# The weighted sum of expert value rows: from half VectorE, half TensorE to TensorE alone

## Chip, core and metric

The kernel runs on one core of a Trainium2 chip. The metric is the device time of one execution in microseconds (us), the median of three runs. All data is fp32.

## What is computed

A two-layer decoder trunk over 256 tokens of width 1024, batch 1. Layer 0 mixes tokens with sparse attention and retention, layer 1 with a convolution module; behind each stands a PEER layer, and at the end a norm. The change touches PEER, in which every token picks 16 experts in each of 8 heads out of 16384, and every expert is one row of `u` and one of `v`:

```python
def block(args):
    xb, ib, gb = args                       # 128 tokens, their 128 picks, their gates
    hb = jnp.einsum('td,tkd->tk', xb, u[ib])
    act = jax.nn.gelu(hb, approximate=False) * gb
    return jnp.einsum('tk,tkd->td', act, v[ib])
```

The picks come from a routing step: queries (`h @ w_q`), scores against 2 x 128 keys, top 16 of each half, top 16 of the sums, softmax.

## The kernel before

**Phases and rounds.** Tokens lie on the 128 partitions, in two tiles. There are four PEER phases p: layer 0 tile 0, layer 0 tile 1, layer 1 tile 0, layer 1 tile 1. A phase has 128 picks, in 8 rounds of RING = 16, a round in 4 batches of BATCH = 4. Every engine has its own program, and semaphores order them.

**One pick.** GpSimd (POOL) issues an indirect DMA that gathers for each token its expert's row, `u` and `v` side by side (2048 fp32, 1 MB for 128 tokens), into slot r of `ring` (L414); at most AHEAD = 5 are under way, and a slot must be free. VectorE makes the dot product with `h_tok` (L892). After four dots ScalarE makes gelu, multiplies by the gate (L566) and writes four diagonal matrices `diag` (L573), eight of which exist. The weighted row is added to the token's sum in two halves: VectorE adds columns 0 to 511 to `x_tok` (`add_v`, L900), four picks behind its dots; TensorE multiplies the diagonal with columns 512 to 1023 and accumulates in PSUM in `acc` (L1284), opened by `open_sum` (L1277) with the identity times `x_tok`, and copied back by `close_sum` (L915). A slot is free when `v_added` and `v_multiplied` have both counted it.

**What runs beside the rounds.** In phase 0 (from round 0), and in the rounds 4 to 7 of phases 1 and 2, the routing of the next picks is made two heads at a time. In TensorE's program a piece stands behind each batch: query 0 behind batch 0, query 1 behind batch 1, scores 0 behind batch 2, scores 1 behind batch 3 (`heads_in_steps`, L1266; products L1042, scores L1263). VectorE's `heads` (L811) stands behind the round's dots and additions and begins with the maxima over both heads' scores (L822); the next round's dots stand behind it. In rounds 0 and 1 of phase 0 TensorE also makes two of the four products of the attention's output projection for tile 1, behind batches 2 and 3, and VectorE adds them (`add_projected`) ahead of round 2. Rounds 0 to 3 of phases 1 and 2 hold the convolution of a tile: TensorE's `conv_in` makes 8 channel tiles behind batches given by CONV_INS, ScalarE their gates by CONV_GATES (L584), VectorE a `conv_pair` of 31 taps for two channel tiles (L931, L943) between rounds or, for pairs 1 and 3, ahead of pick 8 of round 1 and pick 12 of round 2; then mean, variance, norm, and four products `conv_out` with the second weight in round 3. Phase 3 has only picks. Weights (1 MB chunks of 256 columns) come on SyncE's queue into two buffers `wbuf` (L328), each load waiting for the product of the chunk two before it.

Of the kernel before, what the change touches and what calls it, by code (L numbers as in the profile page):

```python
# [6 lines left out]
P = 128  # L7
D = 1024
KD = D // P
# [29 lines left out]
HALF = D // 2  # L39
# [29 lines left out]
def hybrid_decoder_trunk_kernel(nc, x, gains, w_in, kv_norm, uk_t, uv_w, w_o, rot, decay,  # L69
# [13 lines left out]
    with ctx:  # L83
# [125 lines left out]
        acc = side[:, 2, :]  # L209
        cand = side[:, 3, :].rearrange("p (h a b) -> p h a b", h=2, a=P_TOP)  # L210
        pm = ctx.enter_context(nc.psum_tensor("pm", [P, 4 * 512], f32))
# [23 lines left out]
        wo_ps = sem("wo_ps")  # L235
# [5 lines left out]
        dots_ready, act_ready, diag_ready, v_added, v_multiplied = (sem(n) for n in ("dots_ready", "act_ready", "diag_ready", "v_added", "v_multiplied"))  # L241
# [17 lines left out]
        wo_at = [[side_flat[:, c * 512:c * 512 + WCOLS] for c in range(4)], [pm[:, c * 512:c * 512 + WCOLS] for c in range(4)]]  # L259
# [104 lines left out]
        def _(pool):  # L364
# [22 lines left out]
            def gathers(p):  # L387
# [3 lines left out]
                with pool.Fori(0, rounds // 2) as i:  # L391
                    for half in range(2):
                        r0 = p * rounds + half
                        pool.wait_ge(picks_ready, i * 2 + (r0 + 1))
                        pool.wait_ge(v_added, i * (2 * RING) + (r0 * RING + 1))
# [4 lines left out]
                        for r in range(RING):  # L400
                            freed = r0 * RING + r + 1
                            pool.wait_ge(v_added, i * (2 * RING) + freed)
# [20 lines left out]
        def _(act):  # L423
# [155 lines left out]
            def gate_of_glu(t, n):  # L579

                c = n % 4
                act.wait_ge(pw_ps, t * KD + n + 1)
                act.wait_ge(glu_ready, t * KD + n + 1)
                act.activation(gate_sig[:, c, :], pm[:, c * 512 + P:c * 512 + 2 * P], ACT.Sigmoid,  # L584
                               bias=chan_sb[:, CP_BG + n:CP_BG + n + 1]).then_inc(sig_ready, 1)
# [69 lines left out]
        def _(dve):  # L655
# [12 lines left out]
            dve.sem_inc(glu_ready, 4)  # L668
            dve.sem_inc(v_added, RING)
# [114 lines left out]
            def add_projected(t, c):  # L784
# [3 lines left out]
                dve.tensor_tensor(xs, xs, wo_at[t][c], ALU.add)  # L788
# [94 lines left out]
            def expert_round(p, i, between=None):  # L883
# [4 lines left out]
                xs = x_tok[:, t, 0:HALF]  # L888

                def dot(r):  # L890
# [4 lines left out]
                def add_v(r):  # L895
                    n = p * PICKS + r
                    if r % BATCH == 0:
                        dve.wait_ge(act_ready, i * RING + (n + BATCH))
                    dve.wait_ge(v_added, i * RING + (n + RING))
                    dve.scalar_tensor_tensor(out=xs, in0=ring[:, r, D:D + HALF], scalar=act_v[:, r:r + 1], in1=xs,  # L900
                                             op0=ALU.mult, op1=ALU.add).then_inc(v_added, 1)

                for r in range(RING + BATCH):
                    if between:
                        between(r)
                    if r < RING:
                        dot(r)
                    if r >= BATCH:
                        add_v(r - BATCH)  # L910

            def close_sum(p):

                dve.wait_ge(v_multiplied, RING + (p + 1) * PICKS)
                dve.tensor_copy(x_tok[:, p % 2, HALF:D], acc).then_inc(x_ready, 1)  # L915

# [9 lines left out]
            def conv_pair(t, q):  # L926

                tiles = range(2 * q, 2 * q + 2)
                for c in tiles:
                    dve.wait_ge(sig_ready, t * KD + c + 1)  # L930
                    dve.scalar_tensor_tensor(out=glu[:, c, HIST:HIST + P], in0=pm[:, (c % 4) * 512:(c % 4) * 512 + P],  # L931
                                             scalar=chan_sb[:, CP_BA + c:CP_BA + c + 1], in1=gate_sig[:, c % 4, :],
                                             op0=ALU.add, op1=ALU.mult).then_inc(glu_ready, 1)
                for w in range(TAPS):
                    for c in tiles:
                        src, dst = glu[:, c, w:w + P], y_t[:, c, :]
                        tap = chan_sb[:, CP_DW + c * TAPS + w:CP_DW + c * TAPS + w + 1]
                        if w == 0:
                            dve.wait_ge(glu_ready, 4 + t * KD + c + 1)
# [26 lines left out]
            def conv_out(t):  # L966
# [5 lines left out]
                for c in range(4):  # L972
                    n = 4 * t + c
                    dve.wait_ge(w2_ps, n + 1)
                    xs = x_tok[:, t, c * WCOLS:(c + 1) * WCOLS]
                    dve.tensor_tensor(xs, xs, pm[:, c * 512:c * 512 + WCOLS], ALU.add)
# [14 lines left out]
            heads(0, 1)  # L991
            expert_round(0, 1)
            heads(0, 2)
            for c in range(4):
# [35 lines left out]
        def _(pe):  # L1030
# [171 lines left out]
            def output_product(t, c):  # L1202
                pe.wait_ge(a_ready, t + 1)
                pe.wait_ge(b_t_ready, t + 1)
                w = chunk(W_O[t] + c + (t and c // 2 * 2))
# [67 lines left out]
            def open_sum(p):  # L1273
# [3 lines left out]
                pe.matmul(acc, ident[:, :], x_tok[:, p % 2, HALF:D], start=True, stop=False)  # L1277

            def expert_round(p, i, between=None, last=False):

                for r in range(RING):
                    n = p * PICKS + r
                    pe.wait_ge(diag_ready, i * RING + (n + 1))
                    pe.matmul(acc, diag[:, r % (2 * BATCH), :], ring[:, r, D + HALF:2 * D],  # L1284
# [147 lines left out]
```

## Time and profile before

| | us |
|---|---|
| median of 3 runs | 1746.88 |
| lowest, highest | 1746.08, 1751.19 |
| span of the profiled execution | 1750.9 |
| VectorE busy | 1428.1 (82%) |
| TensorE busy (matmul) | 1002.7 (57%) |
| GpSimd, ScalarE busy | 775.9 (44%), 498.4 (28%) |
| DMA | 625.78 MB, 357 GB/s over the span |

DVE is VectorE, PE TensorE (PEld its weight loads), ACT ScalarE, POOL GpSimd, SPq SyncE's DMA queue. A square bracket at the end of a timeline row gives the idle time of the engine just before it and what ended it.
### The profile page before, as it was taken

The numbers are of one execution on the slowest core, as the hardware profiler recorded it, in microseconds if no ns is written. First come the engines' busy times: TensorE is split into PE (matmuls) and PEld (weight loads), VectorE is DVE, ScalarE is ACT, GpSimd is POOL, SyncE is SP. The second block draws the span as 40 slices with busy tenths as digits, with TensorE's granted clock in tenths as the row PEclk, the third lists the DMA queues.
The fourth block names the chain that finished last, engine by engine and source line by source line (L and its number), as shares of the span: only waits on it lengthen the run. The fifth ranks groups of instructions, "written<-read, shape, count | busy, mean of one in ns | idle before, by whom it ended". The sixth has DMA issues, their size and how long they took to land.

```text
span 1750.9 us, 17116 instructions
## 1 busy us (share of the span) xinstructions
PE 1002.7 (57%) x3934; PEld 610.9 (35%) x3934; DVE 1428.1 (82%) x3330; ACT 498.4 (28%) x1442; POOL 775.9 (44%) x565
## 2 busy tenths in 40 slices
PE   7998663555443653465455555355644456555655
PEld 7785442333331331333333333133422332222222
DVE  2755594999999889894999999988599999877776
ACT  2222220333222522232223242223222233222222
POOL 0003431434434578852344448874333345544551
PEclk9999777787777886676777777678777777776777
DMA  9147989799999999898999998899899998999996
GB/s 356 55 133 301 410 303 366 290 379 385 385 384 402 420 364 368 315 393 318 408 389 378 402 371 338 323 341 418 310 382 395 406 394 335 422 422 422 422 422 266
DMA packets 149994, 625.78 MB, mean 357 GB/s; under 512 B 9648, under 2 KB 76976, under 8 KB 84400
## 3 DMA queue, kind: packets, MB, share of 16 engines
q0 software_dynamic: 73728, 536.90, 75.7%
q1 hardware_dynamic: 76208, 88.20, 14.8%
q8 instruction: 24, 0.39, 0.1%
q14 instruction: 34, 0.28, 0.0%
HBM read 624.02 MB, written 1.05 MB: 357 GB/s over the span
## 4 chain that ended last, share of the span: by engine, by line
DVE 43%; PE 20%; DMA 17%; issue 11%; ACT 4%; DVEq 3%; ACTq 1%; POOL 0%; POOLq 0%
DVE ring L892 15%; DMA ring<-experts_dram,idx_now 11%; DVE x_tok L900 9%; PE pm L1042 9%; PE side L1284 7%; DVE conv_buf L943 7%; DMA wbuf<-w_o_dram 3%; DMA wbuf<-w_dram 3%; ACT act_v L566 1%; PE side L1042 1%; DVE top_i L825 1%; DVE rest L826 1%; DVE top_i L838 1%; ACTq L569 1%; DVE best_i L844 1%
## 5 line engine op out<-in xcount | busy, mean ns | idle before, releaser
L414 POOL DMA_INDIRECT ring<-experts_dram,idx_now x512 | 745.4, 1456 | 633.5 <-DMA ring<-experts_dram,idx_now 247.1
L1284 PE MATMUL side<-ring,diag 128*128 128x512 f32 x1024 | 597.0, 737 | 555.7 <-ACT diag L573 555.6
L892 DVE SCALAR_TENSOR_TENSOR ring<-ring,h_tok 128x1024 f32<-128x1024 f32 x512 | 615.7, 1220 | 55.8 <-DMA ring<-experts_dram,idx_now 50.7
L1284 PEld LDWEIGHTS side<-ring,diag 128*128 128x128 f32 x1024 | 232.6, 239 | 863.9 <-ACT diag L573 625.4
L900 DVE SCALAR_TENSOR_TENSOR x_tok<-ring,act_v,x_tok 128x512 f32<-128x512 f32 x512 | 383.8, 750 | 26.1 <-ACT act_v L566 20.3
L562 ACT ACTIVATE ge<-hb 128x4 f32<-128x4 f32 x128 | 26.3, 205 | 701.3 <-DVE ring L892 701.3
L573 ACT ACTIVATE diag<-ident,act_v 128x128 f32<-128x128 f32 x512 | 163.8, 390 | 15.9 <-issue 2.2
L397 POOL COPY idx_now<-eidx 128x16 uint32 x32 | 24.3, 760 | 258.1 <-DVE x_tok L900 184.3
L943 DVE SCALAR_TENSOR_TENSOR conv_buf<-conv_buf,chan_sb 128x128 f32<-128x128 f32 x480 | 126.7, 347 | 0.0
L1042 PEld LDWEIGHTS side<-h_t,wbuf 128*128 128x128 f32 x1024 | 119.3, 192 | 15.3 <-issue 15.3
L1042 PE MATMUL side<-h_t,wbuf 128*128 128x128 f32 x1024 | 119.5, 275 | 0.0
L566 ACT ACTIVATE act_v<-ge,gates 128x1 f32<-128x1 f32 x512 | 109.0, 283 | 15.6 <-issue 10.9
L1042 PE MATMUL pm<-h_t,wbuf 128*128 128x128 f32 x512 | 63.8, 286 | 21.8 <-DMA wbuf<-w_dram 21.8
L1042 PEld LDWEIGHTS pm<-h_t,wbuf 128*128 128x128 f32 x512 | 63.4, 202 | 30.4 <-DMA wbuf<-w_dram 23.5
L553 ACT ACTIVATE expo<-lead 128x16 f32<-128x16 f32 x32 | 6.6, 208 | 227.6 <-DVE lead L853 227.6
L822 DVE MAX8 top_v<-side 128x8 f32<-128x128 f32 x64 | 15.6, 288 | 63.7 <-PE side L1263 63.7
L562 ACT ACT_TABLE_LOAD x46 | 59.0, 1283 | 3.4 <-issue 2.5
L1042 PE MATMUL pm<-conv_buf,ring 128*128 128x128 f32 x448 | 53.7, 280 | 0.2 <-DVE ring L770 0.2
L1042 PEld LDWEIGHTS pm<-conv_buf,ring 128*128 128x128 f32 x448 | 52.3, 194 | 1.4 <-DVE ring L770 0.6
L1042 PE MATMUL pm<-wbuf,h_t 128*128 128x256 f32 x128 | 33.4, 420 | 27.2 <-DMA wbuf<-w_dram 23.1
L1042 PE MATMUL pm<-wbuf,conv_buf 128*128 128x256 f32 x64 | 22.9, 536 | 42.2 <-DMA wbuf<-w_o_dram 42.2
L1036 PE MATMUL pm<-ident,h_tok 128*128 128x128 f32 x56 | 12.6, 405 | 57.5 <-DVE h_tok L663 57.5
(188 smaller groups left out, 838.0 us busy)
## 6 DMA issues: line engine op xcount, KB each, us to landing
wbuf<-wq_dram SPq DMA_DIRECT2D x32, 1024.0 KB, 25.8
wbuf<-w_dram SPq DMA_DIRECT2D x24, 1024.0 KB, 19.8
ring<-w_in_dram SPq DMA_DIRECT2D x5, 2048.0 KB, 20.0
wbuf<-w_o_dram SPq DMA_DIRECT2D x8, 1024.0 KB, 17.1
ring<-experts_dram,idx_now POOLq DMA_INDIRECT x512, 11.5
gain<-gains_dram SPq DMA_DIRECT2D x7, 512.0 KB, 13.9
ring<-w_in_dram SPq DMA_DIRECT2D x1, 1696.0 KB, 10.1
x_tok<-x_dram SPq DMA_DIRECT2D x2, 512.0 KB, 4.7
```

The source lines that it names most:

```text
L397: pool.tensor_copy(idx_now[:, half, :], eidx[:, t, ds(i * (2 * RING) + half * RING, RING)]) \
L414: pool.indirect_dma_start(ring[:, r, :], None, table[layer], bass.IndirectOffsetOnAxis(idx_now[:, half, r:r + 1], 0)) \
L562: act.activation(ge[:, c], hb[:, c], ACT.Gelu)
L566: last = act.activation(act_v[:, r:r + 1], ge[:, r:r + 1], ACT.Copy, scale=gates[:, t, ds(i * RING + r, 1)])
L569: act.drain()
L573: act.activation(diag[:, (b % 2) * BATCH + j, :], ident[:, :], ACT.Copy, scale=act_v[:, r:r + 1]).then_inc(diag_ready, 1)
L825: dve.max_index(top_i[:, b, j, 0:8], top_v[:, b, j, 0:8], side[b, j])
L892: dve.scalar_tensor_tensor(out=ring[:, r, 0:D], in0=ring[:, r, 0:D], scalar=1.0, in1=h_tok[:, t, :], op0=ALU.mult, op1=ALU.mult, accum_out ...
L900: dve.scalar_tensor_tensor(out=xs, in0=ring[:, r, D:D + HALF], scalar=act_v[:, r:r + 1], in1=xs, op0=ALU.mult, op1=ALU.add).then_inc(v_add ...
L943: step = dve.scalar_tensor_tensor(out=dst, in0=src, scalar=tap, in1=dst, op0=ALU.mult, op1=ALU.add)
L1042: last = pe.matmul(dst, lhs(k), rhs(k), start=(k == 0), stop=(k == KD - 1))
L1284: pe.matmul(acc, diag[:, r % (2 * BATCH), :], ring[:, r, D + HALF:2 * D], start=False, stop=(last and r == RING - 1)) \
```

## The change

The first 512 columns of the weighted row are no longer multiplied and added by VectorE. TensorE makes two matmuls for each pick, with the same diagonal, one for each half of the row, and accumulates in two PSUM banks, `acc[0]` and `acc[1]`. VectorE keeps the dots. The semaphore `v_added` goes; POOL waits for `v_multiplied` alone, which counts the second matmul. `open_sum` has two matmuls, `close_sum` two copies. The second accumulator takes a quarter of `pm`, so others make room: the output products of tile 1 share two places in place of four, so VectorE adds the first two ahead of round 1 and TensorE waits for that (`projected_added`) before it writes the other two; `conv_in` alternates between two places in place of four, `glu_ready` starts at 2 in place of 4; `conv_out` puts two chunks in one bank, and VectorE waits for both before it reads one.

The diff, shortened to the changed lines and their neighbours:

```diff
@@ -206,9 +206,9 @@
         ps_q = side[:, 0:2, 2 * P:4 * P]
-        acc = side[:, 2, :]
+        pm = ctx.enter_context(nc.psum_tensor("pm", [P, 4 * 512], f32))
+        acc = [side[:, 2, :], pm[:, 1536:2048]]
         cand = side[:, 3, :].rearrange("p (h a b) -> p h a b", h=2, a=P_TOP)
-        pm = ctx.enter_context(nc.psum_tensor("pm", [P, 4 * 512], f32))
@@ -256,7 +256,7 @@
         a_at = [side_flat[:, 1536:2048], pm[:, 1536:2048]]
-        wo_at = [[side_flat[:, c * 512:c * 512 + WCOLS] for c in range(4)], [pm[:, c * 512:c * 512 + WCOLS] for c in range(4)]]
+        wo_at = [[side_flat[:, c * 512:c * 512 + WCOLS] for c in range(4)], [pm[:, c % 2 * 512:c % 2 * 512 + WCOLS] for c in range(4)]]
@@ -392,14 +392,13 @@
                         pool.wait_ge(picks_ready, i * 2 + (r0 + 1))
-                        pool.wait_ge(v_added, i * (2 * RING) + (r0 * RING + 1))
+                        pool.wait_ge(v_multiplied, i * (2 * RING) + (r0 * RING + 1))
                         pool.sem_inc(may_gather, 1)
...
                             freed = r0 * RING + r + 1
-                            pool.wait_ge(v_added, i * (2 * RING) + freed)
                             pool.wait_ge(v_multiplied, i * (2 * RING) + freed)
@@ -581,7 +580,7 @@
                 act.wait_ge(glu_ready, t * KD + n + 1)
-                act.activation(gate_sig[:, c, :], pm[:, c * 512 + P:c * 512 + 2 * P], ACT.Sigmoid,
+                act.activation(gate_sig[:, c, :], pm[:, c % 2 * 512 + P:c % 2 * 512 + 2 * P], ACT.Sigmoid,
                                bias=chan_sb[:, CP_BG + n:CP_BG + n + 1]).then_inc(sig_ready, 1)
@@ -665,8 +664,7 @@
             dve.sem_inc(s_read, 2)
-            dve.sem_inc(glu_ready, 4)
-            dve.sem_inc(v_added, RING)
+            dve.sem_inc(glu_ready, 2)
             norm(0)
@@ -785,7 +783,7 @@
                 xs = x_tok[:, t, c * WCOLS:(c + 1) * WCOLS]
-                dve.tensor_tensor(xs, xs, wo_at[t][c], ALU.add)
+                dve.tensor_tensor(xs, xs, wo_at[t][c], ALU.add).then_inc(projected_added, 1)
                 if c == 3:
@@ -885,34 +883,21 @@
                 rounds = PICKS // RING
-                xs = x_tok[:, t, 0:HALF]
-
-                def dot(r):
+
+                for r in range(RING):
+                    if between:
+                        between(r)
                     dve.wait_ge(gathered[r], i * 16 + 16 * (p * rounds + 1))
...
-                def add_v(r):
-                    n = p * PICKS + r
-                    if r % BATCH == 0:
-                        dve.wait_ge(act_ready, i * RING + (n + BATCH))
-                    dve.wait_ge(v_added, i * RING + (n + RING))
-                    dve.scalar_tensor_tensor(out=xs, in0=ring[:, r, D:D + HALF], scalar=act_v[:, r:r + 1], in1=xs,
-                                             op0=ALU.mult, op1=ALU.add).then_inc(v_added, 1)
-
-
-                for r in range(RING + BATCH):
-                    if between:
-                        between(r)
-                    if r < RING:
-                        dot(r)
-                    if r >= BATCH:
-                        add_v(r - BATCH)
-
             def close_sum(p):
+                t = p % 2
                 dve.wait_ge(v_multiplied, RING + (p + 1) * PICKS)
-                dve.tensor_copy(x_tok[:, p % 2, HALF:D], acc).then_inc(x_ready, 1)
+                for c in range(2):
+                    last = dve.tensor_copy(x_tok[:, t, c * COLS:(c + 1) * COLS], acc[c])
+                last.then_inc(x_ready, 1)
@@ -928,7 +913,7 @@
                     dve.wait_ge(sig_ready, t * KD + c + 1)
-                    dve.scalar_tensor_tensor(out=glu[:, c, HIST:HIST + P], in0=pm[:, (c % 4) * 512:(c % 4) * 512 + P],
+                    dve.scalar_tensor_tensor(out=glu[:, c, HIST:HIST + P], in0=pm[:, c % 2 * 512:c % 2 * 512 + P],
                                              scalar=chan_sb[:, CP_BA + c:CP_BA + c + 1], in1=gate_sig[:, c % 4, :],
@@ -970,10 +955,9 @@
                 for c in range(4):
-                    n = 4 * t + c
-                    dve.wait_ge(w2_ps, n + 1)
+                    dve.wait_ge(w2_ps, 4 * t + c // 2 * 2 + 2)
                     xs = x_tok[:, t, c * WCOLS:(c + 1) * WCOLS]
-                    dve.tensor_tensor(xs, xs, pm[:, c * 512:c * 512 + WCOLS], ALU.add)
+                    dve.tensor_tensor(xs, xs, pm[:, c * WCOLS:(c + 1) * WCOLS], ALU.add)
                 dve.drain().then_inc(x_ready, 1)
@@ -989,9 +973,11 @@
             heads(0, 1)
+            for c in range(2):
+                add_projected(1, c)
             expert_round(0, 1)
             heads(0, 2)
-            for c in range(4):
+            for c in range(2, 4):
                 add_projected(1, c)
@@ -1202,6 +1188,8 @@
                 pe.wait_ge(b_t_ready, t + 1)
+                if t and c >= 2:
+                    pe.wait_ge(projected_added, 4 + c - 1)
                 w = chunk(W_O[t] + c + (t and c // 2 * 2))
@@ -1274,16 +1262,18 @@
                     pe.wait_ge(x_ready, (0, 3, 5, 7)[p])
-                pe.matmul(acc, ident[:, :], x_tok[:, p % 2, HALF:D], start=True, stop=False)
+                for c in range(2):
+                    pe.matmul(acc[c], ident[:, :], x_tok[:, p % 2, c * COLS:(c + 1) * COLS], start=True, stop=False)
...
                     pe.wait_ge(diag_ready, i * RING + (n + 1))
-                    pe.matmul(acc, diag[:, r % (2 * BATCH), :], ring[:, r, D + HALF:2 * D],
-                              start=False, stop=(last and r == RING - 1)) \
-                        .then_inc(v_multiplied, 1)
+                    for c in range(2):
+                        step = pe.matmul(acc[c], diag[:, r % (2 * BATCH), :], ring[:, r, D + c * COLS:D + (c + 1) * COLS],
+                                         start=False, stop=(last and r == RING - 1))
+                    step.then_inc(v_multiplied, 1)
                     if between and (r + 1) % BATCH == 0:
@@ -1292,7 +1282,7 @@
                 for j in range(2):
-                    last = product(pm[:, (c % 4) * 512 + j * P:(c % 4) * 512 + (j + 1) * P],
+                    last = product(pm[:, c % 2 * 512 + j * P:c % 2 * 512 + (j + 1) * P],
                                    lambda k: w[:, k, j * P:(j + 1) * P], lambda k: h_t[:, k, :])
@@ -1310,7 +1300,7 @@
                 w = chunk(W_CONV[t] + KD + c)
-                dst = pm[:, c * 512:c * 512 + WCOLS]
+                dst = pm[:, c * WCOLS:(c + 1) * WCOLS]
                 product(dst, lambda k: z_t[:, k, :], lambda k: w[:, k, :]).then_inc(w2_ps, 1)
```

## Rows read from the trace of the kernel before

**Rows 1.** The page: busy time of each engine, and the chain by engine.

```profile
PE 1002.7 (57%) x3934; PEld 610.9 (35%) x3934; DVE 1428.1 (82%) x3330; ACT 498.4 (28%) x1442; POOL 775.9 (44%) x565
...
DVE 43%; PE 20%; DMA 17%; issue 11%; ACT 4%; DVEq 3%; ACTq 1%; POOL 0%; POOLq 0%
```

**Rows 2.** Busy time by stretch (A:B, its length, engines), with clock and DMA.

```profile
core 0: us, PE busy (x) PEld busy (x) DVE busy (x) ACT busy (x) POOL busy (x), PEclk, DMA share, GB/s
923.34:948.73 25.39, 25.31 (x104) 15.35 (x104) 23.49 (x40) 9.85 (x33) 14.14 (x11) 0.88 0.92 355
...
1500.00:1700.00 200.00, 113.70 (x162) 43.66 (x162) 153.65 (x242) 54.38 (x189) 99.67 (x86) 0.75 1.01 422
...
917.97:966.24 48.27, 25.31 (x104) 15.35 (x104) 44.76 (x117) 13.15 (x44) 19.96 (x17) 0.75 0.97 382
...
584.00:816.00 232.00, 126.86 (x488) 79.83 (x488) 195.89 (x468) 72.89 (x180) 149.21 (x72) 0.76 0.93 364
```

**Rows 3.** Timeline of TensorE, 895 to 972: start, us, engine, line, operation, count.

```profile
895.92 3.70 PE L1284 MATMUL side<-ring,diag 128*128 128x512 f32 x8 [1.35 <-ACT diag L573]
...
923.34 6.71 PE L1284 MATMUL side<-ring,diag 128*128 128x512 f32 x8 [23.28 <-ACT diag L573]
929.89 3.73 PE L1042 MATMUL side<-h_t,wbuf 128*128 128x128 f32 x32
933.46 3.60 PE L1284 MATMUL side<-ring,diag 128*128 128x512 f32 x8
936.89 3.73 PE L1042 MATMUL side<-h_t,wbuf 128*128 128x128 f32 x32
...
944.59 3.70 PE L1284 MATMUL side<-ring,diag 128*128 128x512 f32 x8
948.12 0.61 PE L1263 MATMUL side<-keys_sb,q_t 128*128 128x128 f32 x4
971.62 6.46 PE L1284 MATMUL side<-ring,diag 128*128 128x512 f32 x8 [22.89 <-ACT diag L573]
```

**Rows 4.** Timeline of VectorE, 923 to 967.

```profile
923.43 1.22 DVE L892 SCALAR_TENSOR_TENSOR ring<-ring,h_tok 128x1024 f32<-128x1024 f32 x1
...
925.24 1.22 DVE L892 SCALAR_TENSOR_TENSOR ring<-ring,h_tok 128x1024 f32<-128x1024 f32 x1
...
947.15 0.49 DVE L822 MAX8 top_v<-side 128x8 f32<-128x128 f32 x2
948.89 0.50 DVE L822 MAX8 top_v<-side 128x8 f32<-128x128 f32 x2 [1.25 <-PE side L1263]
...
965.09 1.23 DVE L892 SCALAR_TENSOR_TENSOR ring<-ring,h_tok 128x1024 f32<-128x1024 f32 x1 [0.25 <-issue]
...
966.24 1.22 DVE L892 SCALAR_TENSOR_TENSOR ring<-ring,h_tok 128x1024 f32<-128x1024 f32 x1
```

**Rows 5.** Timeline, phase 0 round 0: the weight load and the product that waits.

```profile
183.56 7.38 SPq L328 DMA_DIRECT2D wbuf<-w_o_dram  x2
...
209.88 6.73 PE L1042 MATMUL pm<-wbuf,conv_buf 128*128 128x256 f32 x16 [15.46 <-DMA wbuf<-w_o_dram]
```

**Rows 6.** Timeline of TensorE, phase 0 round 7: its first and last batch.

```profile
556.95 5.59 PE L1284 MATMUL side<-ring,diag 128*128 128x512 f32 x8 [22.74 <-ACT diag L573]
...
578.12 3.70 PE L1284 MATMUL side<-ring,diag 128*128 128x512 f32 x8 [1.84 <-ACT diag L573]
```

**Rows 7.** Timeline, phase 1, convolution: VectorE's gate waits, TensorE's wait for weights.

```profile
650.88 0.35 DVE L931 SCALAR_TENSOR_TENSOR conv_buf<-pm,chan_sb,gate_sig 128x128 f32<-128x128 f32 x1 [4.65 <-ACT gate_sig L584]
...
726.21 0.35 DVE L931 SCALAR_TENSOR_TENSOR conv_buf<-pm,chan_sb,gate_sig 128x128 f32<-128x128 f32 x1 [4.37 <-ACT gate_sig L584]
...
801.82 6.03 PE L1042 MATMUL pm<-wbuf,h_t 128*128 128x256 f32 x16 [11.15 <-DMA wbuf<-w_dram]
```

**Rows 8.** Timeline at the end of phase 3: the last batch and the copy.

```profile
1738.85 5.14 PE L1284 MATMUL side<-ring,diag 128*128 128x512 f32 x8 [3.23 <-ACT diag L573]
...
1744.04 0.69 DVE L915 COPY x_tok<-side 128x512 f32<-128x512 f32 x1 [2.54 <-PE side L1284]
```

More of the change, by code:

```diff
@@ L38 @@
 BATCH = 4
-HALF = D // 2
+COLS = D // 2
 WCOLS = 256
@@ L234, in hybrid_decoder_trunk_kernel @@
         p_t_ps, p_t_ready, o_ps, o_ready, a_ps, a_ready = (sem(n) for n in ("p_t_ps", "p_t_ready", "o_ps", "o_ready", "a_ps", "a_ready"))
-        wo_ps = sem("wo_ps")
+        wo_ps, projected_added = sem("wo_ps"), sem("projected_added")
         w_loaded = [sem(f"w_loaded{i}") for i in range(WBUF)]
@@ L240, in hybrid_decoder_trunk_kernel @@
         idx_copied, may_gather = sem("idx_copied"), sem("may_gather")
-        dots_ready, act_ready, diag_ready, v_added, v_multiplied = (sem(n) for n in ("dots_ready", "act_ready", "diag_ready", "v_added", "v_multiplied"))
+        dots_ready, act_ready, diag_ready, v_multiplied = (sem(n) for n in ("dots_ready", "act_ready", "diag_ready", "v_multiplied"))
         pw_ps, sig_ready, glu_ready = sem("pw_ps"), sem("sig_ready"), sem("glu_ready")
@@ L938, in conv_pair @@
                         if w == 0:
-                            dve.wait_ge(glu_ready, 4 + t * KD + c + 1)
+                            dve.wait_ge(glu_ready, 2 + t * KD + c + 1)
                             step = dve.tensor_scalar(dst, src, tap, chan_sb[:, CP_DWB + c:CP_DWB + c + 1], ALU.mult, ALU.add)
```

## The prediction

> **What bounds the kernel now.** I read the page first: VectorE is busy 82% of the span, TensorE 57%, and the chain that ended last runs 43% through VectorE and 20% through TensorE [rows 1]. That alone would call VectorE the bound. So I went on to the stretches. 13 of the 32 rounds of 16 picks have the same shape: in phase 0 rounds 2 to 6, in phases 1 and 2 rounds 4 to 7. Beside the picks TensorE makes the queries and scores of two routing heads, and VectorE turns the scores into picks (`heads`) before it starts the next round. Such a round lasts 48.3 us; VectorE is busy 44.8 of them, the DMA engines 97%, TensorE only 25.3 [rows 2]. But those 25.3 us lie in one block: from its first diagonal matmul at 923.34 to the end of the second scores at 948.73 TensorE is busy 25.31 of 25.39 us [rows 2]. Its timeline says the same: a batch of 4 picks, a query, a batch, a query, a batch, scores, a batch, scores, with hardly a gap; then it is idle for 22.9 us until the next round's first diagonal [rows 3]. VectorE's timeline says why: the maximum over the first head's scores starts at 947.15, the one over the second head's at 948.89, after 1.25 us of waiting for TensorE's scores, and from there `heads` runs without a stop to the next round's first dot product at 965.09 [rows 4]. Two loops are thus closed at almost the same length: VectorE's own work, and TensorE's block, then `heads`, then four dots, then ScalarE, then TensorE's block. VectorE's 1.25 us of waiting says that the second is already the longer one at this point.
>
> **The price of one pick.** A matmul of 128x512 in fp32 is two records in the trace. Four picks are 8 records: from 933.46 to the next query at 936.89 is 3.43 us, and 0.86 us a pick, with the clock at its upper level [rows 3]. The first batch of a round takes 6.71 us, because TensorE was idle 23.3 us before it and the clock is at its lower level [rows 3]; 6.55 us after the start the query runs at the pace that it keeps. The change adds one more such matmul for each pick, with the same diagonal. The weight load hides behind the matmul stream before, and I give it no price. So each batch grows by 4 x 0.86 = 3.44 us. For the first batch I take the same 3.44: the clock rises at the same time after the start, and the added records lie behind that. The bounds are 0 (the rise comes earlier) and 7.0 (all 16 records at the lower level, 13.7 us in all).
>
> **What is removed.** VectorE loses one 128x512 multiply-add per pick. Its dots follow one another every 1.15 us where no multiply-add lies between (965.09, 966.24), and every 1.81 us where one does (923.43, 925.24) [rows 4]: 0.66 us x 512 = 338 us of VectorE. The question is what that is worth. In a round with heads it shortens VectorE's own loop from some 48 us to 16 x 1.15 + 18 = 36 us, and TensorE's loop by nothing but the gap in front of the fourth batch, where TensorE waits for ScalarE's diagonals, and so for the last dots: 1.35 us in the round before this one, under 0.1 in this one [rows 3]; between them I take 0.6.
>
> **The rounds with heads.** The second head's scores stand in TensorE's program behind the fourth batch; `heads` waits for them; the next dots stand behind `heads`; and the next round's diagonals come from these dots. So what is added to TensorE's block is added to the round: 4 x 3.44 - 0.6 = 13.2 us. The block becomes 38.6 us, the round 61.5. Nothing else is late before it: from a round's first dot at 965.09 [rows 4] to its first diagonal matmul at 971.62 [rows 3] are 6.5 us, 4.6 of them dots, so ScalarE is ready 1.9 us after a batch's dots, and the diagonal buffer that it then waits for is the one of two batches ago. DMA needs 46.8 us a round (0.97 x 48.27) [rows 2], which fits into 61.5. POOL now waits for the matmuls alone; it did before too, for the later one. 13 x 13.2 = 172 us.
>
> **Rounds 0 and 1 of phase 0.** There the third batch is followed by an output product that waits for a weight chunk. The load is issued at 183.56, when the round's first query is done, and the product starts at 209.88 [rows 5]. The first batch stands ahead of that query (+3.4), the fourth behind the product (+3.4); the second and third are hidden by the load. 2 x 6.9 = 14 us. If the load is quicker because fewer gathers run beside it, up to 3 us less each. Two of VectorE's four additions of the output product now stand ahead of round 1 in place of round 2; the work is the same and their products are made before `heads` ends. The new wait of TensorE on them, `projected_added`, has round 1's batches behind it, but it is met before that round's first diagonal exists: 0.
>
> **Round 7 of phase 0** has no queries: its first batch starts at 556.95 and the last ends at 581.8 [rows 6], with gaps for VectorE in between. In their place come 9.0 + 3 x 6.88 = 29.7 us: +5. The second copy in `close_sum` costs as much as the first, 0.69 us [rows 8], in phases 0, 1 and 2: +2.
>
> **Phases 1 and 2, rounds 0 to 3 (convolution).** These 232 us hold 196 us of VectorE and 93% DMA [rows 2], so here there is something to gain and something to lose. I placed TensorE's batches anew with 3.44 us more each and VectorE's dots at 1.15 us. In round 0 TensorE reaches the gate of channel tile 1 about when VectorE has come to it today: +0. In round 1 VectorE inserts tiles 2 and 3 at pick 8. It waits there for a gate today already, 4.65 us [rows 7]; it arrives 5 us sooner and TensorE's product (first batch, then `conv_in`) comes 3.4 us later plus the shift of its start: it leaves at +4. Behind `conv_pair` of tiles 4 and 5 (needs all of round 1's third batch) it is at +6. In round 2 the insert of tiles 6 and 7 waits for the product behind the second batch; today 4.37 us of waiting [rows 7], then some 17 us: +13. The four last dots without their multiply-adds give 6 back: +7 at the start of round 3. There TensorE makes the fourth batch and the variance before it can start (+7 again for z), then the first `conv_out` at +13, because the second batch is in front of it. That product releases the load of the third chunk, for which TensorE waits until 801.82 [rows 7]; then the fourth batch costs 3.4 more. +16 at the end of the block, with bounds +5 (the load is faster with fewer gathers beside it) and +25. The glu buffers (2 for 4) bind `conv_in` only one tile behind `conv_pair`, and there TensorE is behind VectorE anyway: 0, at most 4 us, within these bounds. In `conv_out` VectorE's third addition now waits for the fourth product, so one addition of 256 columns moves behind it: less than the 0.69 us of a copy of 512 [rows 8], within the rounding. 2 x 16 = 32 us.
>
> **Phase 3** is bound by DMA: 422 GB/s, share 1.01 for 200 us [rows 2]. Four picks of 1.05 MB at that rate come every 9.9 us. TensorE is busy 113.7 of the 200 us, 5.7 of these 9.9, and then some 7 to 9, so it keeps up. The first slot is given back 1.7 us later, the next ones up to 4: +3. At the end the last batch takes 5.14 us, then 7 to 8.6, and the copy behind it (0.69 us [rows 8]) is made twice: +3. Together +6.
>
> **Sum:** 172 + 14 + 5 + 2 + 32 + 6 = +231 us on a profiled span of 1750.9. The timed runs had a median of 1746.9, 4.0 us below this span, so nothing outside the span needs to be added. 1746.9 + 231 = 1978; I say 1977.
>
> **A rule against this.** The share of VectorE is the highest of the compute engines [rows 1]. The Trainium skill, Perfetto Trace Analysis, Identifying the Most-Contended Engine, says that the engine with the highest occupancy is the most contended and is to be optimized first. By that rule the change takes 338 us from the right engine. The round's own rows disagree: VectorE waits for TensorE there.
>
> **Rivals.**
> *Relief wins, faster.* If the added matmuls hid in TensorE's idle 43%, the DMA engines would be next: 48.3 - 46.8 = 1.5 us saved in 13 rounds, up to 7% of each convolution block (2 x 16), and some 3 at the start: about -55, 1692. For it speaks TensorE's low share. It decides as soon as TensorE's block does not stand between the dots and `heads`; since the second scores stand behind the fourth batch in every one of the 13 rounds, I see no room. 5%.
> *Cheaper second matmul.* Same diagonal, so perhaps the pair costs less than twice one, or the clock rises sooner because TensorE is busier. With 2.3 us a batch in place of 3.44, +150: 1897. Against it: the records follow each other at 0.43 us with the load (0.2 us) already hidden. 8%.
> *First batches wholly at the lower clock.* +3.5 us for each of some 22 first batches and cold restarts in the convolution: +75 on top, 2052. Speaks for it: today's first batches (6.46 and 6.71 us) are nearly all slow [rows 3]. Against: the query behind them runs fast at once [rows 3]. 6%.
>
> **Chances and range.** Forecast 81%. The range 1900 to 2035 holds it with its bounds (13 rounds at 10 to 15 us, the convolution at +5 to +25 each) and half of the cheaper case. A measurement of this kernel tells about 0.3% from no change. Faster 5%, within 0.3% 1%, slower 94%.
>
> **What the trace after would show.** Twice as many records of the diagonal matmul; TensorE's block in a round with heads 38 to 39 us long and without gaps; the time between rounds 61 to 62 us; VectorE waiting some 10 us for scores in each such round, and its share of the span about 55% in place of 82%; DMA share about 0.75 there; phase 3 still at 422 GB/s. Wrong I am if the round stays below 55 us, if the pair of matmuls of a pick takes less than 1.6 us at the upper clock, or if the clock in the block differs from today's 0.88 by more than 0.1.

## The result and the profile after

| | before | after |
|---|---|---|
| median of 4 runs, us | 1749.0 | 1972.0 |
| lowest, highest | 1746.1, 1752.9 | 1967.9, 1977.1 |
| span of the profiled execution | 1750.9 | 1973.9 |

The ratio is 1.127, with a 95% interval of 1.124 to 1.130. The change makes the kernel 12.7% slower; forecast were 1977 us and a slowdown of 13% on a median of 1746.9. (With the further run of the kernel before its median is 1749.0.)

The page of the changed kernel, busy times and the chain by engine, against [rows 1]:

```profile
PE 1380.9 (70%) x4966; PEld 789.3 (40%) x4966; DVE 1082.1 (55%) x2822; ACT 495.3 (25%) x1442; POOL 741.9 (38%) x565
...
PE 49%; DVE 23%; DMA 19%; DVEq 3%; ACT 3%; issue 2%; ACTq 1%; POOL 0%; POOLq 0%
```

VectorE lost 346 us of work and TensorE gained 378. The chain that ended last has gone over from VectorE (43%) to TensorE (49%).

Busy time of the changed kernel by stretch (columns as in [rows 2]): TensorE's block in round 5 of phase 1, that whole round, the first convolution block, 200 us of phase 3.

```profile
987.90:1026.00 38.10, 37.90 (x136) 21.07 (x136) 12.44 (x25) 9.65 (x33) 16.37 (x15) 0.94 0.81 319
...
981.40:1042.50 61.10, 37.91 (x136) 21.08 (x136) 33.80 (x101) 12.96 (x44) 18.24 (x17) 0.81 0.78 310
...
674.90:920.20 245.30, 172.62 (x616) 101.10 (x616) 151.85 (x405) 73.50 (x181) 143.88 (x70) 0.83 0.88 343
...
1700.00:1900.00 200.00, 160.06 (x333) 66.22 (x332) 99.75 (x162) 54.33 (x189) 103.26 (x86) 0.93 1.01 422
```

The same round in TensorE's timeline, which answers to [rows 3] (one row is now one matmul):

```profile
987.89 2.08 PE L1274 MATMUL side<-ring,diag 128*128 128x512 f32 x2 [23.40 <-ACT diag L572]
989.76 1.91 PE L1274 MATMUL pm<-ring,diag 128*128 128x512 f32 x2
991.47 1.40 PE L1274 MATMUL side<-ring,diag 128*128 128x512 f32 x2
992.71 1.02 PE L1274 MATMUL pm<-ring,diag 128*128 128x512 f32 x2
...
997.00 3.73 PE L1028 MATMUL side<-h_t,wbuf 128*128 128x128 f32 x32
1000.57 1.02 PE L1274 MATMUL side<-ring,diag 128*128 128x512 f32 x2
1001.43 1.02 PE L1274 MATMUL pm<-ring,diag 128*128 128x512 f32 x2
...
1007.44 3.73 PE L1028 MATMUL side<-h_t,wbuf 128*128 128x128 f32 x32
...
1017.88 0.61 PE L1251 MATMUL side<-keys_sb,q_t 128*128 128x128 f32 x4
...
1025.19 0.61 PE L1251 MATMUL side<-keys_sb,q_t 128*128 128x128 f32 x4
1048.99 1.22 PE L1274 MATMUL side<-ring,diag 128*128 128x512 f32 x1 [23.19 <-ACT diag L572]
```

And in VectorE's, against [rows 4]:

```profile
1018.63 0.50 DVE L820 MAX8 top_v<-side 128x8 f32<-128x128 f32 x2 [18.84 <-PE side L1251]
1025.95 0.50 DVE L820 MAX8 top_v<-side 128x8 f32<-128x128 f32 x2 [6.82 <-PE side L1251]
1042.47 1.23 DVE L891 SCALAR_TENSOR_TENSOR ring<-ring,h_tok 128x1024 f32<-128x1024 f32 x1 [0.59 <-issue]
```

From 987.89 to 1025.8 TensorE has no gap. A pick costs 0.86 us twice (1000.57, 1001.43, then the next). VectorE has finished its 16 dots 19 us before the first scores come, and then waits 6.82 us more for the second: that is the fourth batch, 4 x 1.72 us. From the second maximum to the next dot it is 16.5 us, and 16.2 before: `heads` itself is unchanged.

I took the start of each round's first dot from VectorE's timeline in both traces. The stages between them:

| stage | before | after | difference | forecast |
|---|---|---|---|---|
| up to the first dot | 167.7 | 174.8 | +7.1 | none |
| phase 0, rounds 0 and 1 | 139.4 | 150.8 | +11.4 | +14 |
| phase 0, rounds 2 to 6 | 243.5 | 306.6 | +63.1 | +66 |
| phase 0, round 7 | 36.5 | 42.7 | +6.2 | +5.7 |
| phase 1, rounds 0 to 3 (convolution) | 232.4 | 245.3 | +12.9 | +16 |
| phase 1, rounds 4 to 7 | 195.9 | 247.3 | +51.4 | +53.5 |
| phase 2, rounds 0 to 3 (convolution) | 231.4 | 247.5 | +16.1 | +16 |
| phase 2, rounds 4 to 7 | 195.6 | 246.8 | +51.1 | +53.5 |
| phase 3 and the end | 308.5 | 312.1 | +3.6 | +6 |

The first row is not the change's: its code is the same, and the eleven other traces of this study have their first dot between 166.1 and 169.7. What made this one late stays open. The other rows sum up to +216 us where +231 were forecast. So part of the close hit, 1972 for 1977, is luck: in the trace, 7 us that nobody forecast stand in for half of the 15 that the stages gave less.

### The profile page after: what moved, and what is told of

It reads as the page before. It is cut to its first block, busy times and chain, and to the rows that moved or that the text cites. A ratio compares the mean times of both kernels' runs of the same rounds, so it can differ in the third digit from the quotient of the medians.

```text
span 1973.9 us, 17815 instructions
## 1 busy us (share of the span) xinstructions
PE 1380.9 (70%) x4966; PEld 789.3 (40%) x4966; DVE 1082.1 (55%) x2822; ACT 495.3 (25%) x1442; POOL 741.9 (38%) x565
## 4 chain that ended last, share of the span: by engine, by line
PE 49%; DVE 23%; DMA 19%; DVEq 3%; ACT 3%; issue 2%; ACTq 1%; POOL 0%; POOLq 0%
PE side L1274 16%; PE pm L1274 15%; DMA ring<-experts_dram,idx_now 14%; PE pm L1028 9%; DVE conv_buf L928 6%; DVE ring L891 6%; PE side L1028 6%; DMA wbuf<-w_o_dram 3%; DMA wbuf<-w_dram 3%; DVE top_i L823 1%; DVE rest L824 1%; DVE top_i L836 1%; ACT act_v L565 1%; PE side L1251 1%; DVE best_i L842 1%
## 5 line engine op out<-in xcount | busy, mean ns | idle before, releaser
L413 POOL DMA_INDIRECT ring<-experts_dram,idx_now x512 | 712.1, 1391 | 679.8 <-PE pm L1274 379.0
L1274 PE MATMUL side<-ring,diag 128*128 128x512 f32 x1024 | 575.1, 645 | 450.3 <-ACT diag L572 450.3
L891 DVE SCALAR_TENSOR_TENSOR ring<-ring,h_tok 128x1024 f32<-128x1024 f32 x512 | 598.5, 1224 | 146.7 <-DMA ring<-experts_dram,idx_now 141.6
L1274 PE MATMUL pm<-ring,diag 128*128 128x512 f32 x1024 | 553.3, 623 | 0.0
L1274 PEld LDWEIGHTS side<-ring,diag 128*128 128x128 f32 x1024 | 200.9, 206 | 688.7 <-ACT diag L572 484.5
L1274 PEld LDWEIGHTS pm<-ring,diag 128*128 128x128 f32 x1024 | 207.9, 203 | 272.2 <-issue 272.2
L565 ACT ACTIVATE act_v<-ge,gates 128x1 f32<-128x1 f32 x512 | 109.0, 283 | 15.6 <-issue 11.5
L546 ACT COPY q_t<-side 128x256 f32<-128x256 f32 x32 | 11.9, 372 | 235.3 <-PE side L1028 235.3
L1028 PE MATMUL pm<-h_t,wbuf 128*128 128x128 f32 x512 | 59.7, 275 | 0.0
L916 DVE SCALAR_TENSOR_TENSOR conv_buf<-pm,chan_sb,gate_sig 128x128 f32<-128x128 f32 x16 | 5.6, 352 | 96.8 <-ACT gate_sig L583 96.8
```

Source lines behind the costliest of these rows:

```text
L413: pool.indirect_dma_start(ring[:, r, :], None, table[layer], bass.IndirectOffsetOnAxis(idx_now[:, half, r:r + 1], 0)) \
L565: last = act.activation(act_v[:, r:r + 1], ge[:, r:r + 1], ACT.Copy, scale=gates[:, t, ds(i * RING + r, 1)])
L891: dve.scalar_tensor_tensor(out=ring[:, r, 0:D], in0=ring[:, r, 0:D], scalar=1.0, in1=h_tok[:, t, :], op0=ALU.mult, op1=ALU.mult, accum_out ...
L1028: last = pe.matmul(dst, lhs(k), rhs(k), start=(k == 0), stop=(k == KD - 1))
L1274: step = pe.matmul(acc[c], diag[:, r % (2 * BATCH), :], ring[:, r, D + c * COLS:D + (c + 1) * COLS], start=False, stop=(last and r == RING ...
```

## The experiments

The theory is one loop: TensorE's block of a round (picks, queries, scores), then `heads`, then four dots and ScalarE. Its rivals are that VectorE's work sets the time, or the amount of TensorE's work wherever it stands. "A round with heads" below is the usual distance of first dots in the 13 rounds: 48.6 us before, 61.2 after (the expectations have 48.7).

**The matmul without the relief.** `add_v` is back in VectorE's loop, into a scratch tile:

```diff
+                xs = onehot[:, :, :, :, :].rearrange("p a b c d -> p (a b c d)")[:, 0:512]
...
+                    dve.scalar_tensor_tensor(out=xs, in0=ring[:, r, D:D + 512], scalar=act_v[:, r:r + 1], in1=xs,
+                                             op0=ALU.mult, op1=ALU.add).then_inc(v_added, 1)
```

> The changed kernel, and VectorE makes its 512-column multiply-add for every pick again (into a scratch tile, its result is not used); the slots wait for it as before. So the cost of the second matmul stands alone, without the relief of VectorE. Theory (TensorE's block and `heads` in one loop): a round with heads takes 61 us, VectorE's own work in it 48 us at most, so it fits again: 0 there and in phase 3; only the convolution gives some of it back, 5 to 10 us a block. 1985 us, between 1972 and 2000. Rival (the relief is worth its 338 us of VectorE time, or a good part): 2070 or more.

Measured: 1992.8 us, ratio to before 1.140 (1.137 to 1.143). One of its rounds with heads:

```profile
986.60:1047.80 61.20, 38.09 (x136) 21.20 (x136) 44.94 (x116) 12.95 (x44) 20.90 (x17) 0.81 0.78 309
```

VectorE is busy 11.1 us more than in the changed kernel's round, and the round is as long as that one. In these rounds the relief is worth nothing beside the second matmul. The convolution blocks are 13 and 10 us longer (258.5, 257.8), a little more than expected. The whole relief of 346 us is worth 21 us (25 in the traces from the first dot on), and the rival is out.

**The relief without the matmul.** Half of the columns is left out:

```diff
-                    for c in range(2):
+                    for c in range(1):
                         step = pe.matmul(acc[c], diag[:, r % (2 * BATCH), :], ring[:, r, D + c * COLS:D + (c + 1) * COLS],
```

> The changed kernel without the second matmul of each pick: half of the columns of the weighted sum is left out. So the relief of VectorE stands alone. Theory: TensorE's block is back at 25 us, less the gap before the fourth batch; a round with heads 47.7 us, 0.6 under the kernel before, and DMA (46.8) is next to it; the convolution blocks gain 5 to 15 us each. 1720 us, between 1695 and 1740; the second matmul then costs about 250 us. Rival (VectorE was the bound): 338 us of its time go, as far as DMA allows, 1650 or less.

Measured: 1734.7 us, ratio 0.992 (0.990 to 0.994). A round with heads, and the two products of the convolution's end that wait for weights:

```profile
860.00:907.30 47.30, 24.09 (x104) 14.97 (x104) 33.78 (x100) 12.96 (x44) 18.64 (x18) 0.75 1.00 395
```

```profile
780.57 6.07 PE L1028 MATMUL pm<-wbuf,h_t 128*128 128x256 f32 x16 [14.48 <-DMA wbuf<-w_dram]
...
802.16 5.52 PE L1028 MATMUL pm<-wbuf,h_t 128*128 128x256 f32 x16 [12.09 <-DMA wbuf<-w_dram]
```

The round is 47.3 us as expected, with DMA at a share of 1.00. So the second matmul costs 1972.0 - 1734.7 = 237 us. The convolution block is where I was wrong: 241.7 and 230.1 us, where 232 less 5 to 15 was expected. Rounds 0 to 2 are faster (160 us for 168), round 3 is slower (82 for 65). TensorE now comes to the last two weight chunks earlier and waits for both; the kernel before waited for one of them [rows 7].

**The scores ahead of the fourth batch.** The same work in another order:

```diff
-                else:
-                    scores(p, i, n - 2)
+                elif n == 2:
+                    scores(p, i, 0)
+                    scores(p, i, 1)
```

> The changed kernel with the same work, but TensorE makes the second head's scores right behind the first head's, ahead of the fourth batch. Theory: `heads` no longer waits for the fourth batch, so its 6.9 us leave the loop of each of the 13 rounds (61.2 to 54.3 us): -90; rounds 0 and 1 of phase 0 lose some 12 each, since `heads` starts before the output product. 1860 us, between 1845 and 1885. Rival (TensorE's amount of work sets the time): no change, 1972.

Measured: 1866.9 us, ratio 1.068 (1.066 to 1.070).

```profile
904.90:959.10 54.20, 37.92 (x136) 20.91 (x136) 33.70 (x101) 12.96 (x44) 18.38 (x17) 0.85 0.88 353
```

TensorE is busy 37.9 us as in the changed kernel's round, and the round is 54.2 us long in place of 61.2: the fourth batch has left the loop (7.0 us, and it is 6.9 long). Rounds 0 and 1 lost 14 us each. So it is not the amount of TensorE's work as such that sets the time, but how much of it stands between the dots and the end of `heads`.

What I overlooked, in the prediction too: only 11 of the 13 rounds have this loop alone. In round 7 of phases 1 and 2 `close_sum` stands behind the dots, and it waits for the last matmul of the fourth batch wherever the scores are. These two rounds gained nothing (64.6 and 63.9 us, 64.1 and 63.6 in the changed kernel), so it is 1867 and not 1860. The wait ahead of that copy, in the changed kernel and here:

```profile
1147.85 0.69 DVE L899 COPY x_tok<-side 128x512 f32<-128x512 f32 x1 [26.03 <-PE pm L1274]
```

```profile
1058.10 0.69 DVE L899 COPY x_tok<-side 128x512 f32<-128x512 f32 x1 [26.51 <-PE pm L1275]
```

**All routing ahead of the first batch.**

```diff
+            def route(p, i):
+                for b in range(2):
+                    queries(p, i, b)
+                for b in range(2):
+                    scores(p, i, b)
...
+                route(1, i)
-                expert_round(0, i + 3, lambda b: heads_in_steps(1, i, b))
+                expert_round(0, i + 3)
```

> The changed kernel with the same work, but TensorE makes both queries and both scores of a round ahead of its first batch, while it waits for VectorE anyway, and ScalarE copies the queries there. Theory: `heads` waits for no batch of its round; VectorE's own loop is 36 us, TensorE's work 39, DMA's 46.8, so a round takes 47 to 50 us in place of 61.2: -165 with a further -25 in rounds 0 and 1 of phase 0: 1782 us, between 1765 and 1815, DMA share of such a round over 0.93. Rival (TensorE's amount of work sets the time): no change, 1972.

Measured: 1754.1 us, ratio 1.003 (1.002 to 1.005); 218 us of the loss are back without a matmul less. Two rounds with heads:

```profile
845.10:892.10 47.00, 44.61 (x164) 24.64 (x163) 34.34 (x101) 14.22 (x45) 20.96 (x18) 1.00 1.02 416
892.10:938.20 46.10, 35.76 (x122) 20.45 (x122) 34.18 (x100) 14.10 (x45) 19.71 (x17) 0.89 1.02 410
```

DMA is full and the bound of these rounds, as the prediction's faster rival had it. I expected 1782. The 13 rounds gave back 180 us in place of 165: the usual one takes 46.5 us, and the first of a group of four only 38, in which no dot waits for a gather and DMA's share is 0.72. The last round of phases 1 and 2 still takes 61 us, for the reason above. Rounds 0 and 1 gave 35 in place of 25, and 7 us are the early first dot (168.2), which is not this edit's.

**The same order in the kernel before.** The edit is the one above, made in the kernel before.

> The kernel before (VectorE adds half of each weighted row) with the same reorder as in the run with routing first: both queries and both scores of a round ahead of its first batch. Theory: VectorE's own work is then the longest loop of a round with heads, 31.6 us of dots and additions and 16.4 of `heads`: 47.5 in place of 48.7 us, -16 in 13 rounds; rounds 0 and 1 of phase 0 gain some 12 each as `heads` starts ahead of the output product. 1707 us, between 1690 and 1725; then the change is slower in this order too, by what it costs in the convolution and in the rounds without heads. Rival (once TensorE is out of the loop, the relief of VectorE decides): this one is slower than the changed kernel in the same order, over 1754.

Measured: 1769.7 us, ratio 1.009 (1.006 to 1.012). The theory's number (1707) fell and its rival came true: this order is faster with the change than without, 1754.1 to 1769.7. Its round 4 of phase 1 and the next, and VectorE in that round 4:

```profile
823.80:881.10 57.30, 38.53 (x184) 27.11 (x184) 44.74 (x118) 18.73 (x50) 20.37 (x17) 0.86 0.89 346
881.10:928.30 47.20, 28.35 (x104) 16.39 (x104) 44.63 (x117) 14.39 (x45) 19.68 (x17) 0.79 1.01 399
```

```profile
839.72 0.75 DVE L910 SCALAR_TENSOR_TENSOR x_tok<-ring,act_v,x_tok 128x512 f32<-128x512 f32 x1 [10.09 <-ACT act_v L571]
```

The usual round is 47.2 us, near the 47.5 that I had. What I missed are four rounds of 57 to 61 us, rounds 2 and 3 of phase 0 and round 4 of phases 1 and 2. In the one taken apart ScalarE waits for the queries before it makes the first batch's `act_v` (its copies of the queries start at 833.21 and 836.78), and VectorE, whose additions stand between its dots, waits with it. In the changed kernel VectorE needs nothing from ScalarE for its dots and goes on. So this pair does not compare VectorE's speed with TensorE's; it shows that this order does not suit the split of the kernel before.

**The convolution's tiles ahead of the batches, in both kernels.** `conv_in` is made in pairs, the output products in pairs too:

```diff
+                for c in {(0, 0): (0, 1), (1, 0): (2, 3), (1, 2): (4, 5), (2, 0): (6, 7)}.get((i, b), ()):
+                    conv_in(t, c)
...
-                    for c in ((0,), (1, 2), (3,))[b - 1]:
+                elif (i, b) in ((3, 1), (3, 3)):
+                    for c in range(b - 1, b + 1):
                         conv_out(t, c)
```

> The changed kernel with routing first, and in the convolution rounds TensorE makes the channel tiles in pairs ahead of the batches where it idles (0 and 1 before round 0, 2 and 3 before round 1, 4 and 5 before round 1's third batch, 6 and 7 before round 2), ScalarE their gates there, and the output products 0 and 1 together as soon as z is there, 2 and 3 behind the last batch. Theory: the convolution's 245 us are waits of VectorE for gates (97 us in all in the changed kernel) and of TensorE for one weight chunk with a batch behind it; without them DMA (216 us) is next: 222 us a block, -45: 1710 us, between 1690 and 1735. Rival (the block is long because TensorE has more work in it): within 5 us of 1754.

> The kernel before with both reorders, so that it differs from the run ahead of this one by the change alone. Theory: VectorE (196 us in a block of 232) and DMA (216) leave some 6 us a block to gain: 1695 us, between 1680 and 1715. If the relief of VectorE pays at last where neither TensorE's order nor the gates hold it back, the changed kernel in the same order is the faster of the two; I expect it within 20 us, and not faster.

Measured: 1745.1 us with the change, ratio 0.996 (0.993 to 0.999), and 1783.3 us without it, 1.018 (1.013 to 1.022). Both expectations were too low, and against the second one the kernel with the change is the faster, by 38 us. Without it the block takes 241.8 and 238.5 us, 233.0 and 231.6 with routing first alone. With the change, rounds 0 to 2 of the first block take 157 us in place of 171, and round 3 takes 87 in place of 74. I put that down to the moved output products and ran the change with them where they stood:

> The changed kernel with routing first and the channel tiles in pairs ahead of the batches, but the convolution's output products where they stood. The run with these moved too had rounds 0 to 2 of a convolution block in 157 us in place of 171, and round 3 in 87 in place of 74, since both remaining weight chunks were loaded at once. Theory: 157 + 74 = 231 us a block in place of 245: 1726 us, between 1712 and 1742. Rival (the gates were not the wait, DMA takes back what they give): 1745 or more.

Measured: 1742.9 us, ratio 0.996 (0.994 to 0.997), so this fell as well; its rival, that DMA takes back what the gates give, is the nearer one. Round 3 is as long with the products in their old place, and TensorE's timeline shows where:

```profile
774.18 6.37 PE L1042 MATMUL pm<-wbuf,h_t 128*128 128x256 f32 x16 [14.31 <-DMA wbuf<-w_dram]
795.22 6.09 PE L1042 MATMUL pm<-wbuf,h_t 128*128 128x256 f32 x16 [7.80 <-DMA wbuf<-w_dram]
```

As in the run with one matmul, whoever brings the block's first rounds forward waits longer for the weight chunks. Round 3 with routing first alone, and in this run:

```profile
733.65:807.17 73.52, 52.75 (x160) 30.66 (x160) 28.01 (x51) 21.09 (x52) 25.14 (x22) 0.86 0.94 371
```

```profile
719.09:806.44 87.35, 58.73 (x160) 33.28 (x160) 28.76 (x52) 21.14 (x52) 32.95 (x29) 0.79 1.02 411
```

DMA is full for the whole of the longer round, and the last chunk is there 35.3 us after its issue (759.90 to 795.22), 18.8 with routing first alone. That the gathers of the next round are what holds it up is argued from this, not tried.

**The reorders that fit the kernel before.** First the scores alone (the edit of the third experiment), then with the channel tiles in pairs:

> The kernel before with the second head's scores ahead of the fourth batch, alone. Theory: VectorE's own work (47.4 us) is the longest loop of a round with heads in place of TensorE's (48.7): -16; rounds 0 and 1 of phase 0 lose 10 to 14 each, as in the changed kernel: 1711 us, between 1695 and 1735. Against the changed kernel with the same edit (1867) the second matmul then costs 156 us. Rival (VectorE's loop is not the one behind): under 1690 or no change.

> The kernel before with the second head's scores ahead of the fourth batch and the channel tiles in pairs ahead of the batches, the output products where they stood. Nothing stands ahead of a group's first batch here, so VectorE's additions do not wait for ScalarE there, as they did 10 us in the run of before with routing first. Theory: 226 us a convolution block in place of 232, and the gain of the run with the scores alone: 1700 us, between 1685 and 1725.

Measured: 1713.9 us, ratio 0.980 (0.977 to 0.982), and 1711.1 us, ratio 0.979 (0.975 to 0.983). A round with heads is 47.3 us in both. The first came out within 3 us of its expectation, though rounds 0 and 1 of phase 0 did not lose 10 to 14 us each: round 0 became 22.5 us shorter, round 1 1 us longer. The second missed 1700 by 11 (its blocks are 227.8 and 230.7 us, 231.0 and 232.2 with the scores alone), and by their intervals the two can't be told apart. These are the fastest versions of the study, 2% under the kernel before, and they keep VectorE's half. With the scores ahead the two splits stand at 1713.9 and 1866.9: the change costs 153 us in this order, 156 were expected.

## Why the prediction was right

*What bounds the kernel: right.* VectorE's 82% was a share of work with another loop of the same length beside it. The run with the additions back and the run with one matmul part them: 346 us of VectorE's work are worth 21 and 14 us of time, the matmul 237 to 244. Another bound stood close by in each (TensorE's block in the first, DMA at a share of 1.00 in the second), so this is the worth of the relief in this order, not in every one.

*The price of a pick: right.* 0.86 us a matmul, twice, with the weight load hidden. The first batch lasts 9.11 us (987.89 to 997.00), forecast from [rows 3] were 6.71 + 3.44 = 10.15: the clock rose some 4.5 us after the start in this round, 6.5 in that one.

*Rounds with heads: the mechanism right, the size 5% too large.* Measured are 165.6 us in 13 rounds, 1.4 of them copies: 12.6 each, forecast 13.2. The block is 37.9 us long, not 38.6. The gap ahead of the fourth batch was 0.8 us in the mean of the 13 rounds, rather than 0.6; the rest are a few tenths spread over the block. The round that I took apart was the shortest of the 13 before, 48.3 us where the usual one is 48.6: it had no such gap, and a first batch (6.55 us to the query) at the long end of 5.0 to 6.6.

*Rounds 0 and 1, round 7: right within 3 us.* The batches behind the load are hidden as forecast; the product that waited until 209.88 [rows 5] starts at 220.97, of which 7 us are the later start and 4 the longer first batch.

*Convolution: sum right (+12.9 and +16.1, forecast 16), the places within 3 us.* The gate waits of VectorE in the changed kernel, against 4.65 and 4.37 us [rows 7]:

```profile
741.32 0.35 DVE L916 SCALAR_TENSOR_TENSOR conv_buf<-pm,chan_sb,gate_sig 128x128 f32<-128x128 f32 x1 [10.56 <-ACT gate_sig L583]
...
814.00 0.35 DVE L916 SCALAR_TENSOR_TENSOR conv_buf<-pm,chan_sb,gate_sig 128x128 f32<-128x128 f32 x1 [5.25 <-ACT gate_sig L583]
824.44 0.35 DVE L916 SCALAR_TENSOR_TENSOR conv_buf<-pm,chan_sb,gate_sig 128x128 f32<-128x128 f32 x1 [10.09 <-ACT gate_sig L583]
```

In round 2 they sum up to 15.3 us where I had 17. The first block is at +5 at the start of round 2 (forecast +6), at +4 at the start of round 3 (+7) and at +13 at its end (+16). TensorE's wait for the third chunk is still there, 14.96 us.

*Phase 3: right.* Bound by DMA at 422 GB/s as before. The last batch and the two copies:

```profile
1959.27 1.13 PE L1274 MATMUL side<-ring,diag 128*128 128x512 f32 x2 [2.77 <-ACT diag L572]
...
1966.44 0.69 DVE L899 COPY x_tok<-side 128x512 f32<-128x512 f32 x1 [9.02 <-PE pm L1274]
1967.05 0.68 DVE L899 COPY x_tok<-pm 128x512 f32<-128x512 f32 x1
```

From the last batch's start to the first copy it is 7.2 us for 5.2 [rows 8], and the second copy adds 0.6, so the end took +2.6 of its 3. The late slots cost 1 us where I had 3.

*What was wrong.* VectorE waits 25.7 us for scores in a round, not 10: without its additions it arrives 18.8 us early for the first head's scores too. The prediction's own figures say so, a round of 61.5 us less 36 of VectorE's own work. It changes no sum. The last rounds of phases 1 and 2 are not held by the scores, but by `close_sum`, as the run with the scores ahead shows; since that waits for the same fourth batch, they still grew by 13.8 and 13.5 us, a copy included, so this too hid in the sum. And the rival "relief wins" had a wrong price: the run with routing first has the 46 us rounds that it asks for, but ends at 1754 and not at 1692, since the convolution blocks stay at 245 us, round 7 of phase 0 at 42 and that of phases 1 and 2 at 61. The rival of a cheaper second matmul is refuted by the rows (0.86 us and 0.86 us), and so is that of first batches wholly at the lower clock (9.0 to 9.7 us, not 13.7).

*The rule on the busiest engine* (the Trainium skill, Perfetto Trace Analysis, Identifying the Most-Contended Engine: of the compute engines the one with the highest occupancy first) would have taken 338 us off the right engine here; the runs show 14 to 21 us for it in these two orders. The same page of the Trainium skill (Optimization Strategy) also says to find what the busiest engine's gaps wait for, and here that is the better half: the 1.25 us in [rows 4] named TensorE.

## What to carry to other kernels

A high share of busy time does not make an engine the bound: follow one period of the loop through every engine and add up what stands in a row; an engine at half share may have no slack in it at all. Work that is moved onto such a block costs nearly its full length, once per period (12.6 of 13.8 us a round here). Where a product is queued in that block can be worth as much as who computes it: two scores ahead of one batch gave 105 us with the change and 35 without, all routing ahead of the first batch 218 with it. Whether a split between engines pays depends on the order around it, so compare splits in the best order of each. Of the orders tried here the best without the change takes 1711 us and the best with it 1743, so VectorE's half is worth keeping; an order that would suit the changed kernel better was not found, which does not show that there is none.

## What the runs showed of the hardware that I had not expected

TensorE's clock in phase 3. Before, TensorE makes a batch in 5.2 to 6.8 us, idles 3.2 to 4.8 between batches, and is granted 0.75 of its clock over 200 us [rows 2]. With twice the matmuls and the same period it idles 1.1 to 2.8 us, is granted 0.93, and makes a batch in 7.1 us, or in 8.8 where part of it runs at the lower level. So for double the work its busy time went from 113.7 to 160.1 us, not to 227. This fits what the Trainium skill, TensorE: Matmul & The Clock Gate, The HAM clock gate, says, that activity releases a throttle that is the default.

The load of a weight chunk of 1 MB for which TensorE comes to wait takes 24 to 26 us beside the gathers (from 183.56 to 209.88 in [rows 5], 24.3 us ahead of the product at 801.82 in [rows 7], 26.0 and 25.1 us in the changed kernel, 25.2 with routing first), with DMA at a share of 1.01 to 1.02 in these stretches. The load issued behind it is less steady: 18.2 us in the changed kernel's round 3, 35.3 with the channel tiles in pairs. TensorE's wait for the third output chunk of a convolution block stands in every run of this study, between 7.5 and 15.6 us long; no order tried here took it away.
